# Two-layer diffusion backbone with expert retrieval: the opening and the last stage lead with token tile 0, context tile 0 moves into an earlier stage, and the modulation matmuls use four column tiles

## The chip, the cores and the metric

One core of a Trainium2 chip runs the whole forward pass as one program. The metric is the device time of that program in microseconds (us). The program is written out by hand: every engine (TensorE = PE, VectorE = DVE, ScalarE = ACT, GpSimd = POOL, SyncE = SP) has its own in-order list of instructions, and they meet at semaphores.

## The reference, cut to what matters

Batch 1, 256 latent tokens and 256 context tokens of width 1024, two layers, all in float32.

```python
for l in range(2):
    ada_x = (silu(c) @ w_ada[l] + b_ada[l])        # six vectors of 1024: modulation; ada_c the same from c_ctx
    hx = modulate(rms_norm(x, norm1_g[l]), ada_x[0], ada_x[1])
    hc = modulate(rms_norm(ctx, norm1_g[l]), ada_c[0], ada_c[1])
    # layer 0: short conv and gated chunk MLP on x and on ctx
    # layer 1: conformer conv, and differential attention of x over [ctx; x]; no new ctx
    yx, yc = mixer(hx, hc)
    x = x + ada_x[2] * yx
    x = x + ada_x[5] * peer(modulate(rms_norm(x, norm2_g[l]), ada_x[3], ada_x[4]))
    # layer 0: the same two lines for ctx

def peer(h):    # for each token: 8 heads x 16 experts out of 16384
    s = product_key_scores(h @ wq)                 # 2 x 128 scores per head
    idx, g = top16(s), softmax(...)
    act = gelu(sum(h * u_tab[idx])) * g
    return sum(act * v_tab[idx])                   # 128 gathered rows of u and v for each token
```

## The kernel before

**Tiles and stages.** Tokens lie on the 128 partitions, so each stream has two tiles (0 and 1). The three uses of `peer` are three stages: stage 0 is x in layer 0, stage 1 is ctx in layer 0, stage 2 is x in layer 1. A stage has 256 slots, 128 for tile 0 and then 128 for tile 1. In one slot POOL issues an indirect gather (L771) that brings one row of 2048 floats (u and v of one expert) to each of the 128 partitions, 1 MB in all, into one of eight ring rows `uv`. DVE multiplies the u half with the token and sums it (L1265), ACT makes the weight and a diagonal matrix of it (L902, L904, L906), and two slots later PE adds the v half to the accumulator with four matmul instructions (L716, `add_values`). POOL may refill a ring row once PE has used it (`uv_used`), and it needs `idx`, the chosen experts of the next head: head h feeds slots 16h to 16h+15 of each tile.

**What makes idx.** For a head: `query` (two groups of 8 matmuls, L548), `score` (L693), and `find`, a chain of small DVE instructions in six parts (L1207 to L1243). `find` runs for one tile or for both at once. `idx` is written at L1237.

**Order of the work.** `schedule()` writes one list that all engines walk. The list `before` (L148) has what runs ahead of a stage's first slot, with nothing gathered meanwhile: the *opening* ahead of stage 0 (modulation of layer 0 as ten `ada` pairs, mixer of x, out projection, first head), and ahead of stage 2 what I call the *last opening* (context norm, context keys and values, attention of 8 tile-heads, out projection, norm, first head). Everything else is `placed`: `spread` deals steps over slots by the costs in `SHARE`, and they run between the slots, while rows are gathered. Each engine takes its steps in list order, so a step that waits holds up the slots behind it on that engine.

**Weights.** SP loads the 118 weight blocks (1 MB each) in the order of first use. There are three slots in `wring`, and in the opening the eight rows of `uv` serve as well. A block's slot is free when its matmuls are done (`multiplied`, L739). POOL's first gather waits once for the last block that lies in `uv` (L777). Behind a query block SP also loads that head's keys, and waits for the `score` of two heads back (L745).

**Modulation.** `ada_pair` (L472) multiplies two blocks with `silu_c`, two columns wide (own and context vector): 16 matmuls of 128x256, which the compiler makes 32 instructions, the two blocks in two column positions (output partitions 0 and 32) at the same time. DVE copies two pieces of two partitions (L942, L943), `ada_turn` (L489) turns them with four matmuls (eight instructions).

**Attention** (L600 and L1138): for each of 8 tile-heads, PE makes scores (L615), DVE a maximum (L1143), ACT the exponentials (L842), DVE the difference of the two softmaxes (L1153), PE turns it (L623), ACT copies it, PE multiplies with the values (L629), and DVE scales the result into `orow` (`take_values`, L1134) before it mixes the next one.

## Time and profile before

| | |
|---|---|
| median of 3 runs | 2508.52 us (2507.24 to 2511.49) |
| the profiled execution, its own time | 2511.18 us |
| its span in the profile | 2509.4 us |
| first gather of stage 0 issued at | 220.08 us |
| last gathers of stage 1 landed, stage 2's first one issued | about 1689 us and 1842.68 us |
| HBM read | 935.88 MB |

How to read it: the span of the profile is what its stretches add up to; the time of an execution is 1.8 us longer, for what lies around the span. All times of rows are counted from the span's start. Busy times of engines overlap.

### The profile page before, as it was taken

Reading aid. Unit: us, or ns where it says so; the run is one execution under the profiler, and the core shown is the slowest. Engines: PE = TensorE matmul, PEld = TensorE weight load, DVE = VectorE, ACT = ScalarE, POOL = GpSimd, SP = SyncE. Lnnn points to the kernel's source line nnn. Section 1 sums busy time; section 2 is a strip of 40 time slices with the busy share of each in tenths; the row PEclk is TensorE's granted clock in tenths of the full one; section 3 lists DMA queues with packets and bytes.
Section 4 is the critical chain, followed back from the end, with each engine's and each line's share of the span. In section 5 each row is a group of like instructions: output and inputs, shape, how many; then the busy total and the mean of one; then the engine's idle time right before and its main releaser. Section 6 shows DMA issues by size and latency. Waiting matters only on the chain.

```text
span 2509.4 us, 23860 instructions
## 1 busy us (share of the span) xinstructions
PE 2162.3 (86%) x6888; PEld 1134.4 (45%) x6888; DVE 1557.4 (62%) x3791; ACT 907.8 (36%) x2688; POOL 1036.9 (41%) x868
## 2 busy tenths in 40 slices
PE   6997998889999978889799898897679987778777
PEld 4775544336655534444365443336455432222222
DVE  1326787775465568867847867454478887544444
ACT  1003343343233444433453334232234443333333
POOL 0002344344444444533434443420025445677774
PEclk9999999999999999999999999998789999999999
DMA  9516999999999999999999999982179999999997
GB/s 398 222 63 241 420 421 418 421 421 421 405 418 420 407 421 414 416 421 406 422 421 412 421 421 416 415 352 70 36 285 420 421 421 421 421 422 422 421 417 325
DMA packets 132304, 938.35 MB, mean 374 GB/s; under 512 B 14688, under 2 KB 17760, under 8 KB 18656
## 3 DMA queue, kind: packets, MB, share of 16 engines
q0 software_dynamic: 110592, 805.36, 77.7%
q1 hardware_dynamic: 21600, 131.63, 13.1%
q8 instruction: 55, 0.90, 0.1%
q14 instruction: 57, 0.47, 0.0%
HBM read 935.88 MB, written 1.05 MB: 373 GB/s over the span
## 4 chain that ended last, share of the span: by engine, by line
PE 41%; DMA 26%; DVE 13%; POOL 9%; issue 8%; ACT 3%; POOLq 0%; SPq 0%; DVEq 0%; ACTq 0%
DMA uv<-uv_dram,stage_idx 25%; PE psum L716 19%; PE psum L548 10%; POOL uv L771 8%; PE psum L535 6%; DVE uv L1265 5%; PE psum L482 2%; PE psum L665 1%; DMA uv<-ada_dram 1%; ACT diag L906 1%; DVE work L1231 1%; ACT wv L904 1%; DVE work L1233 0%; PE psum L496 0%; PE psum L629 0%
## 5 line engine op out<-in xcount | busy, mean ns | idle before, releaser
L716 PE MATMUL psum<-uv,diag 128*128 128x512 f32 x3072 | 1465.0, 617 | 258.2 <-ACT diag L906 251.0
L771 POOL DMA_INDIRECT uv<-uv_dram,stage_idx x768 | 1002.9, 1306 | 1069.1 <-PE psum L716 858.0
L1265 DVE CUSTOM_DVE_ANT_0 uv<-uv,h 128x1024 f32<-128x1024 f32 x768 | 931.7, 1224 | 543.8 <-DMA uv<-uv_dram,stage_idx 531.7
L716 PEld LDWEIGHTS psum<-uv,diag 128*128 128x128 f32 x3072 | 561.7, 193 | 1055.5 <-ACT diag L906 543.4
L902 ACT ACTIVATE gel<-dots 128x1 f32<-128x1 f32 x768 | 155.1, 202 | 1110.4 <-DVE dots L1265 1105.4
L906 ACT ACTIVATE diag<-const,wv 128x128 f32<-128x128 f32 x768 | 308.3, 401 | 25.0
L548 PE MATMUL psum<-hT,wring 128*128 128x256 f32 x1248 | 287.9, 386 | 3.7 <-ACT hT L811 3.7
L548 PEld LDWEIGHTS psum<-hT,wring 128*128 128x128 f32 x1248 | 241.6, 194 | 64.5 <-issue 29.5
L904 ACT ACTIVATE wv<-gel,gw 128x1 f32<-128x1 f32 x768 | 226.3, 295 | 24.9
L763 POOL COPY stage_idx<-idx 128x8 uint32 x96 | 33.9, 353 | 380.5 <-DVE idx L1237 379.8
L793 ACT ACTIVATE work<-psum 128x256 f32<-128x256 f32 (+1 forms) x110 | 47.0, 429 | 177.7 <-PE psum L548 138.1
L482 PE MATMUL psum<-wring,silu_c 128*2 128x256 f32 x544 | 69.6, 395 | 2.2 <-DMA wring<-ada_dram 2.2
L942 DVE COPY ada_rows<-psum 2x256 f32<-2x256 f32 x24 | 9.9, 411 | 96.6 <-PE psum L482 96.6
L1175 DVE TENSOR_TENSOR work<-psum,gate_mix 128x256 f32<-128x256 f32 (+1 forms) x24 | 12.3, 513 | 86.4 <-PE psum L535 57.1
L1265 DVE DVE_READ_ACCUMULATOR2_ANT dots<- 128x1 f32 x768 | 62.6, 82 | 0.0
L535 PE MATMUL psum<-wring,hT 128*128 128x256 f32 x256 | 57.9, 379 | 0.0
L535 PEld LDWEIGHTS psum<-wring,hT 128*128 128x128 f32 x256 | 48.6, 190 | 13.4 <-issue 7.4
L1068 DVE SCALAR_TENSOR_TENSOR work<-work,const 128x256 f32<-128x256 f32 x120 | 50.0, 477 | 0.0
L902 ACT ACT_TABLE_LOAD x38 | 48.8, 1283 | 0.7
L482 PE MATMUL psum<-uv,silu_c 128*2 128x256 f32 x224 | 33.3, 414 | 16.6 <-DMA wring<-ada_dram 10.9
L482 PEld LDWEIGHTS psum<-wring,silu_c 128*2 128x2 f32 x544 | 25.6, 87 | 44.7 <-issue 18.2
L1207 DVE MAX8 work<-work 128x8 f32<-128x128 f32 x96 | 21.2, 278 | 35.2 <-ACT work L793 35.1
(166 smaller groups left out, 1297.0 us busy)
## 6 DMA issues: line engine op xcount, KB each, us to landing
wring<-ada_dram SPq DMA_DIRECT2D x34, 1024.0 KB
wring<-in_dram SPq DMA_DIRECT2D x27, 1024.0 KB
wring<-wq_dram SPq DMA_DIRECT2D x24, 1024.0 KB
uv<-ada_dram SPq DMA_DIRECT2D x14, 1024.0 KB, 8.6
uv<-uv_dram,stage_idx POOLq DMA_INDIRECT x768
uv<-in_dram SPq DMA_DIRECT2D x7, 1024.0 KB, 22.0
uv<-out_w_dram SPq DMA_DIRECT2D x4, 1024.0 KB, 6.0
wring<-out_w_dram SPq DMA_DIRECT2D x4, 1024.0 KB
```

The source lines that it names most:

```text
L482: last = mm(bank[32 * i:32 * i + 2, 0:BLK], silu_c[:, k, :], kc(("ada", i))[:, k, :], start=(k == 0), stop=(k == KC - 1))
L535: last = mm(bank[:, 0:BLK], src[:, k, t * P:(t + 1) * P], w[:, k, :], start=(k == 0), stop=(k == KC - 1))
L548: last = mm(bank[:, 0:TOK], w[:, k, i * P:(i + 1) * P], hT[:, k, :], start=(k == 0), stop=(k == KC - 1))
L716: last = mm(acc[:, b, :], diag[:, s % RING, :], uv[:, s % RING, D + 512 * b:D + 512 * (b + 1)], start=(c == 0), stop=(c == NSEL - 1))
L763: nc.gpsimd.tensor_copy(stage_idx[:, half, :], idx[:, stage % 2, t, bass.ds(it * TOPK + half * RING, RING)]).then_inc(staged, 1)
L771: nc.gpsimd.indirect_dma_start(out=uv[:, s, :], out_offset=None, in_=tables[stage // 2], in_offset=bass.IndirectOffsetOnAxis(ap=stage_idx[ ...
L793: mine.emptied(f(dst, src, func, **kw))
L902: f(gel[:, r:r + 1], dots[:, r:r + 1], ACT.Gelu_apprx_tanh).then_inc(gelu_ready, 1)
L904: f(wv[:, r:r + 1], gel[:, r:r + 1], ACT.Copy, scale=gw[:, (T // TT) % 2, T % TT, c:c + 1]).then_inc(wv_ready, 1)
L906: f(diag[:, r, :], C("ident"), ACT.Copy, scale=wv[:, r:r + 1]).then_inc(diag_ready, 1)
L1068: ops = [v.scalar_tensor_tensor(out=ccT[:, j, :], in0=cpT[:, j, k:k + TOK], scalar=w[:, j, k:k + 1], in1=ccT[:, j, :], op0=ALU.mult, op1=A ...
L1265: v.tensor_tensor_reduce(out=uv[:, r, 0:D], in0=uv[:, r, 0:D], in1=h2[:, stage % 2, t, :], scale=1.0, scalar=0.0, op0=ALU.mult, op1=ALU.ad ...
```

## The change

1. **Opening, tile 0 first.** The out projection runs for tile 0 alone (`out_rows(0, 0)`), then come norm, turn back, query, score and find of head 0 for tile 0 (128 tokens), and then the out projection's remaining blocks, norm and turn back of tile 1. The query of head 1 (first half) is the last step ahead of slot 0.
2. **Last opening, tile 0 first.** Context tile 0 leaves it: its norm, key rows (`kc0`) and value rows (`vc0`) stand in stage 1's slots 131 to 246, beside `k_rows` and `x_rows`, and use the same weight blocks. Only context tile 1 stays. After attention step 5 come tile 0's out projection, norm and query, between the attention steps of tile 1; then score and find of tile 0; then the rest for tile 1.
3. **First heads by tile** (`heads_by_tile`): in stages 0 and 2, heads 0 to 2 of tile 1 are found apart from those of tile 0, within slots 6 to 30. `idx_ready` becomes one semaphore for each tile.
4. **Four column tiles for modulation.** `silu_c` is padded with zeros to 32 columns; `ada_pair` still has 16 matmuls, now in four column positions, each for half of the contraction of one block. One DVE copy of 128x256 takes the place of two small ones; `ada_turn` is two matmuls against a 0/1 matrix that also adds the halves.
5. **Attention:** ACT scales the values into `orow` in place of DVE, through its own ring of banks; from head 3 of tile 0 on the scores have one pair of banks, so that DVE's three banks are free for the out projection.
6. **Smaller ones:** the `spatial` steps are dealt among `ah_cols` and `ac_cols`; some scratch tiles move; `gate(2, 1)` goes from slots 20 to 40 to slots 40 to 60.

The core of the diff:

```diff
-        0: ada(0, 0, 2) + ... + gate(0, 0)
-        + project_out(0)[:4] + ada(0, 8, 9) + project_out(0)[4:] + rms(0) + ada(0, 9, 10) + [("mods", 0, 1)] + norm(0, 1)
-        + first_heads(0),
+        0: ada(0, 0, 2) + ... + gate(0, 0) + deal(out_rows(0, 0), ada(0, 8, 10)) + [("mods", 0, 1)]
+        + rms(0, (0,)) + out_rows(0, 1)[:1] + norm(0, 1)[:1] + [("turn_back", 0, 0)] + query(0, 0, (0,)) + score(0, 0, (0,))
+        + find(0, 0, (0,)) + out_rows(0, 1)[1:]
+        + rms(0, (1,)) + norm(0, 1)[1:] + [("turn_back", 0, 1)] + query(0, 1)[:1],
+        2: rms(1, (1,)) + [("norm_ctx", 2, 1)] + [("kc1", 2, b, 0) for b in range(2)] + [("kc_norm", 2, 1)]
+        + [("vc1", 2, b, 0) for b in range(2)] + [("kc_turn", 2, 1)]
+        + [("attend", 2, i) for i in range(HEADS + 2)] + [("o_norm", 2, 0), ("o_turn", 2, 0)]
+        + [("out_half", 2, 1, 0, 0), ("attend", 2, HEADS + 2), ("out_half", 2, 1, 1, 0)] + rms(2, (0,))
+        + [("attend", 2, HEADS + 3)] + norm(2, 1)[:1] + [("turn_back", 2, 0)] + query(2, 0, (0,))[:1]
+        + [("attend", 2, TT * HEADS), ("o_norm", 2, 1)] + query(2, 0, (0,))[1:] + [("o_turn", 2, 1)] + score(2, 0, (0,))
+        + find(2, 0, (0,)) + [("out_half", 2, 1, b, 1) for b in range(2)]
+        + rms(2, (1,)) + norm(2, 1)[1:] + [("turn_back", 2, 1)] + query(2, 1)[:1],
...
+def heads_by_tile(stage):
+    one, two = (0,), (1,)
+    return [(0, 6, query(stage, 1)[1:] + score(stage, 1, one) + find(stage, 1, one)),
+            (6, 12, query(stage, 0, two) + score(stage, 0, two) + find(stage, 0, two)),
+            (12, 18, query(stage, 2) + score(stage, 2, one) + find(stage, 2, one)),
+            (18, 24, score(stage, 1, two) + find(stage, 1, two) + query(stage, 3)),
+            (24, 30, score(stage, 2, two) + find(stage, 2, two) + query(stage, 4) + score(stage, 3)),
+            (30, 39, next_head(stage, 3))]
...
-                for k in range(KC):
-                    for i in range(2):
-                        last = mm(bank[32 * i:32 * i + 2, 0:BLK], silu_c[:, k, :], kc(("ada", i))[:, k, :],
-                                  start=(k == 0), stop=(k == KC - 1))
+                for k in range(KC // 2):
+                    for q in range(QUAD):
+                        i, kq = q // 2, q % 2 * (KC // 2) + k
+                        last = mm(bank[QW * q:QW * (q + 1), 0:BLK], silu_c[:, kq, :], kc(("ada", i))[:, kq, :],
+                                  start=(k == 0), stop=(k == KC // 2 - 1))
...
-                pool.wait_ge(idx_ready, it * TT + (stage * PH * TT + t + 1))
+                pool.wait_ge(idx_ready[t], it + (stage * PH + 1))
...
-                if i > 1:
-                    take_values(i - 2)
...
+                    empty(orow[:, t, h * P:(h + 1) * P], P, scale=prec[:, (i - 1) % 2, 0:1])
```

## Rows read from the trace of the kernel before

**Rows 1.** The page: busy shares and the span in 40 slices.
```profile
PE 2162.3 (86%) x6888; PEld 1134.4 (45%) x6888; DVE 1557.4 (62%) x3791; ACT 907.8 (36%) x2688; POOL 1036.9 (41%) x868
...
DMA  9516999999999999999999999982179999999997
```
**Rows 2.** Windows, core 0: start:end, length, busy of PE, PEld, DVE, ACT, POOL, PEclk, DMA share, GB/s.
```profile
0.00:220.00 220.00, 188.91 (x1040) 141.81 (x1040) 60.98 (x189) 26.30 (x52) 0.39 (x5) 0.96 0.53 207
220.00:1690.00 1470.00, 1320.78 (x4098) 686.12 (x4099) 1001.09 (x2435) 581.16 (x1732) 636.74 (x575) 0.97 1.01 415
1690.00:1842.00 152.00, 112.67 (x503) 85.30 (x501) 65.67 (x151) 41.93 (x93) 0.19 (x1) 0.85 0.17 59
1842.00:2485.00 643.00, 524.61 (x1218) 216.06 (x1219) 418.87 (x1004) 252.08 (x790) 397.89 (x287) 0.98 1.01 419
```
**Rows 3.** Waits by total, of the two gatherless stretches: POOL.
```profile
POOL stage_idx L763 <- DVE idx L1237: 218.4, 1, 218.4
POOL stage_idx L763 <- DVE idx L1237: 161.4, 1, 161.4
```
**Rows 4.** Timeline of PE in the opening: start, duration, instruction.
```profile
158.74 3.62 PE L482 MATMUL psum<-uv,silu_c 128*2 128x256 f32 x32
163.38 1.05 PE L496 MATMUL psum<-const,ada_rows 2*128 2x2 f32 x8 [1.01 <-DVE ada_rows L943]
144.83 13.98 PE L535 MATMUL psum<-uv,work 128*128 128x256 f32 x64
187.51 1.97 PE L519 MATMUL psum<-const,work 128*128 128x128 f32 x16
```
**Rows 5.** Timeline of PE: two column positions start side by side.
```profile
119.33 0.38 PE L482 MATMUL psum<-uv,silu_c 128*2 128x256 f32 x1
119.34 0.38 PE L482 MATMUL psum<-wring,silu_c 128*2 128x256 f32 x1
119.55 0.38 PE L482 MATMUL psum<-uv,silu_c 128*2 128x256 f32 x1
```
**Rows 6.** Timeline of DVE: find of one tile, from its first to its index instruction.
```profile
209.82 0.49 DVE L1207 MAX8 work<-work 128x8 f32<-128x128 f32 x2 [18.34 <-ACT work L793]
218.42 0.17 DVE L1237 SCALAR_TENSOR_TENSOR idx<-work 128x16 uint32<-128x16 f32 x1
```
**Rows 7.** Timeline of POOL: first gather, ninth and sixteenth.
```profile
220.08 1.09 POOL L771 DMA_INDIRECT uv<-uv_dram,stage_idx  x1 [1.04 <-issue]
234.20 0.96 POOL L771 DMA_INDIRECT uv<-uv_dram,stage_idx  x1 [3.53 <-PE psum L716]
261.60 0.94 POOL L771 DMA_INDIRECT uv<-uv_dram,stage_idx  x1 [5.42 <-PE psum L716]
```
**Rows 8.** Timeline of PE in the last opening, and of DVE at the first find.
```profile
1705.39 30.83 PE L535 MATMUL psum<-wring,uv 128*128 128x256 f32 x128 [1.57 <-ACT uv L811]
1737.84 0.71 PE L615 MATMUL psum<-h 64*128 64x256 f32 x4 [0.74 <-ACT uv L793]
1768.76 0.66 PE L623 MATMUL psum<-const,uv 128*128 128x128 f32 x4 [3.84 <-DVE uv L1153]
1789.20 16.03 PE L665 MATMUL psum<-wring,work 128*128 128x512 f32 x32 [0.69 <-ACT work L793]
1815.77 7.14 PE L548 MATMUL psum<-hT,wring 128*128 128x256 f32 x32 [1.58 <-ACT hT L811]
...
1832.39 0.68 DVE L1207 MAX8 work<-work 128x8 f32<-128x128 f32 x2 [16.72 <-ACT work L793]
```
**Rows 9.** The DMA view of 1690 to 1842 us.
```profile
DMA packets 1734, 9.00 MB, mean 59 GB/s; under 512 B 192, under 2 KB 704, under 8 KB 704
```
**Rows 10.** Windows, the first 100 us of gathers in stages 0 and 2, and stage 1's end.
```profile
220.00:320.00 100.00, 86.97 (x303) 47.16 (x304) 79.22 (x257) 37.35 (x108) 42.57 (x41) 0.95 1.01 416
1842.00:1942.00 100.00, 84.16 (x249) 46.73 (x250) 86.84 (x279) 40.16 (x118) 47.71 (x44) 0.93 0.99 407
1420.00:1690.00 270.00, 240.55 (x713) 112.02 (x712) 163.18 (x309) 102.11 (x308) 107.48 (x100) 0.96 1.00 408
```

More of the change, by code:

```diff
@@ L103, in project_even @@
     return (blocks_of(stage, "v_rows") + [("v_sum", stage)] + blocks_of(stage, "u_cols")[:2] + [("v_scale", stage)]
-            + blocks_of(stage, "u_cols")[2:] + blocks_of(stage, "ah_cols", "ac_cols")
-            + [("spatial", stage, t, j) for t in range(TT) for j in range(MC)] + blocks_of(stage, "ab_cols"))
-def project_out(stage):
-    return blocks_of(stage, "out_rows", n=D // BLK)
-def query(stage, h):
-    return [("query", stage, h, q) for q in range(2)]
-def find(stage, h, tiles):
+            + blocks_of(stage, "u_cols")[2:]
@@ L117, in find, with out_rows, query, score @@
+            + deal(blocks_of(stage, "ah_cols", "ac_cols"), [("spatial", stage, t, j) for t in range(TT) for j in range(MC)])
+            + blocks_of(stage, "ab_cols"))
+def out_rows(stage, t):
+    return [("out_rows", stage, b, t) for b in range(D // BLK)]
+def query(stage, h, tiles=(0, 1)):
+    return [("query", stage, h, q, tiles) for q in range(2)]
+def score(stage, h, tiles=(0, 1)):
+    return [("score", stage, h, tiles)]
+def find(stage, h, tiles=(0, 1)):
     return [("find", stage, h, tiles, part) for part in range(FIND_PARTS)]
@@ L526, in wait_hT, with token_major @@
                 pe.wait_ge(dve_took, n["hT"][1])
-            def token_major(banks, src, what, t):
-                if t == 0:
+            def token_major(banks, src, what, new, done):
+                if new:
                     weights(what)
@@ L534, in token_major, with tile, channel_major @@
                 for k in range(KC):
-                    last = mm(bank[:, 0:BLK], src[:, k, t * P:(t + 1) * P], w[:, k, :], start=(k == 0), stop=(k == KC - 1))
+                    last = mm(bank[:, 0:BLK], src[:, k, :], w[:, k, :], start=(k == 0), stop=(k == KC - 1))
                 banks.fill(last)
-                if t == TT - 1:
+                if done:
                     block_done(what, banks)
-            def channel_major(banks, what, i):
+            def tile(src, t):
+                return src[:, :, t * P:(t + 1) * P]
+            def channel_major(banks, what, i, tiles=(0, 1)):
+                tokens = slice(tiles[0] * P, (tiles[-1] + 1) * P)
                 if i == 0:
                     wait_hT()
-                    weights(what)
+                    if tiles[0] == 0:
+                        weights(what)
                 bank = banks.open(pe)
@@ L598, in qk_turn, with attention_scores @@
                 turn_heads(qk[:, t, :])
+            def attention_scores(i):
+                t, h = i // HEADS, i % HEADS
+                for m in range(2):
+                    half = slice(m * HD, (m + 1) * HD)
+                    for k, keys_of in enumerate((kxT, kcT)):
+                        last = mm(score_bank(i)[:, m, k * TOK:(k + 1) * TOK], qT[half, h, t * P:(t + 1) * P],
+                                  keys_of[half, h, :], start=True, stop=True)
+                last.then_inc(scores_full, 1)
             def attend(stage, i):
@@ L1188, in find @@
             def find(stage, h, tiles, part):
-                if part == 0 and tiles[0] == 0:
-                    n.up("scores")
-                k = n["scores"]
+                k = stage * PH + h + 1
                 a, b = tiles[0], tiles[-1] + 1
@@ L1329 @@
         "lam": rows_(f(d_lambda)),
+        "gather_sums": np.stack([[p // QW // 2 == i and p % QW == v for i in range(2) for v in range(2)] for p in range(P)])
+        .astype(np.float32),
         "b_spatial": np.repeat(f(b_spatial_b)[0].reshape(MC, 2, P).transpose(1, 0, 2), P // 2, axis=0).reshape(P, -1),
```

315 lines of the change are left out of this document (167 added, 148 removed).

## The prediction

> **What bounds the kernel now.** I read the page first: TensorE is busy 86% of the span, yet the line of DMA digits is at 9 everywhere except in slices 2 to 4 and around slice 29 [rows 1]. The windows say why. From 220 to 1690 us and from 1842 to 2485 us the DMA engines are full at 415 and 419 GB/s; in the opening they move 207 GB/s and between 1690 and 1842 us only 59 GB/s [rows 2]. In these two stretches nothing is gathered: the waits of POOL show that it stood 218.4 and 161.4 us for DVE's first index [rows 3]. So the time is (a) the two stretches ahead of a first index, set by a chain over PE, DVE and ACT, (b) bytes divided by some 417 GB/s, (c) a tail. A block or a gathered row of 1.049 MB costs 2.5 us at this rate. A change is worth what it takes off (a), less the blocks that were loaded in (a) and then have to be loaded in (b), plus what it makes (b) lose. The bytes themselves stay: 118 blocks and 768 gathers.
>
> **Opening, modulation.** One `ada` pair takes PE 3.62 us for 32 instructions, 113 ns each [rows 4]. The trace shows two column positions 10 ns apart and a new pair of instructions every 0.21 us [rows 5]; a lone stream of the same shape takes 13.98 / 64 = 218 ns for each [rows 4]. Going from one to two positions thus halved the time; no row shows four. Bounds: 1.8 us a pair (16 instructions' time halved again) to 3.62 us (no gain), or somewhat above. I take 1.8, since the nearest rows are themselves a doubling that worked. DMA sets pairs 0 to 3, of which only the last counts (1.8 plus its turns and copies, 3.0 together); pairs 4 to 7 give 4 x 1.8 = 7.3. `ada_turn` halves from 1.05 us [rows 4]: four of them, 2.0. Dealing out `spatial` saves a PE stall of 0.8. Up to the out projection: 13.1 us earlier.
>
> A rule speaks against this. The Trainium skill (TensorE: Matmul & The Clock Gate, Part 1) says that the sequencer may need about 62 ns for every matmul; counted for the weight loads too that would be 64 x 62 ns = 4.0 us a pair however many positions there are. By that sentence the pair would gain nothing and the opening would be some 12 us longer than I say.
>
> **Opening, tile 0 first.** From the start of the out projection (144.83) to the norm's transposes (187.51) the old path takes 42.7 us [rows 4]. The new one: four out steps and the first of tile 1, 5 x 3.5; two pairs, 3.6; two turns, 1.0; together 22, so 20.7 less. The norm statistics of tile 0 (about 3 us) lie beside tile 1's first step. From the transposes to the start of find (209.82) it was 22.3 us [rows 4, 6]. New: 8 transposes 1.0, their modulation 1.7, turning back 1.0, the query as 32 instructions of 128 columns at 1.97/16 = 0.123, 3.9, and copies and score 1.6: 9.2, so 13.1 less. Find itself stays at 8.6 us [rows 6]. Sum: 13.1 + 20.7 + 13.1 = 47, first gather near 173 instead of 220.
>
> The single wait of POOL for a block in `uv` moves to the third out block, which PE finishes for tile 1 near 169, while DVE still searches until 171.5. That cover is only 2 us. `idx_ready` split in two costs nothing: each tile's finds are in order on DVE.
>
> **Last opening.** Eight context steps take 30.83 us [rows 8]; four stay, near 3.85 each. With one tile less in the norm (2.7) attention begins 19 us earlier. From the first score (1737.84) to find (1832.39) the old path is 94.5 us [rows 8], of it 51.4 attention up to the out projection. Now attention of both tiles is still ahead of find, since tile 1's last steps stand before score; but tile 1's out projection, norm and query are not. Attention 51.4, less 1.6 as the scaling leaves DVE's serial chain; out projection of tile 0, 2 x 4.0; two adds 2.8; norm statistics 2.9; norm 2.7; turning back 1.0; query 3.9; score and copies 1.6: 72.7. DVE handles tile 1's softmax between these in program order and PE idles at every turn; the transposed probability of step 5 waited 3.84 us already [rows 8], and PEclk is 0.85 in this stretch [rows 2], that is, partly at the lower of its two levels. I allow 0 to 9 us for it and take 4, giving 77, so 17.5 less. Sum: 36, bounds 30 to 42. ACT's 0.35 us for each scaling lies beside DVE's maximum of the next step.
>
> **Blocks loaded later.** The old opening moves 207 GB/s x 220 us = 45.5 MB: constants, inputs and 40 blocks. At 173 us the new one has 36, because two query blocks stay held in the three slots: 4 x 2.5 = 10 us go back. Between 1690 and 1842 us 9.00 MB move [rows 9], 8 blocks; the new stretch loads 4, and 2 more beside find, when tile 1's out steps free their slots: 5 us go back (up to 10). Net so far: 47 + 36 - 15 = 68 us.
>
> **What the gather phase loses.** In the first 100 us of gathers DVE is busy 79.2 us in stage 0 and 86.8 in stage 2 [rows 10]. The change adds tile 1's adds, statistics and modulation, about 7 us, and finds by single tile where two were found at once, under one more find of 9.2 us; I take 6. DVE then stands at 92 and 100 of 100 us, with waits on top: find of head 1 can't begin before query 1 is done on PE, near 190 us, ten us behind its first dot. Against it stands the ring: eight rows are issued in 10 us and take 20 us to land, and in the old start DMA stayed full (416 GB/s) though rows 9 to 16 were issued only every 3.9 us [rows 7, 10]. I take 7 us lost in each of the two starts, bounds 0 and 18.
>
> The first query block of head 0 is held until slot 7, so the second block of `ada` pair 10 is issued only then, and SP's next query block and keys queue behind it; PE waits there about 5 us (1 MB at half the rate) with the values of slot 7 behind it. Eight rows in flight cover this: nothing, up to 5 if they have run out. In stage 2 query block 1 likewise waits for tile 1's out projection; its cover is the norm of tile 1.
>
> Stage 1 gets four more steps of 3.5 us on PE (14 us), and norm, transposes and copies of one context tile; the fourteen later pairs give back 1.8 us each. PE is at 240.6 of 270 us there [rows 10]; slack is 29 us, and DMA there runs at 408. I take 1 us, bounds -3 and 10. `gate(2, 1)`, the moved scratch tiles and the dealt `spatial` of stage 1 cost nothing: closing tile 0 needs the gate only at slot 128.
>
> **Sum.** 68 - 14 - 1 = 53 us off. The sum is against the profiled execution: 2511.2 - 53 = 2458. The median lies 2.7 us below that execution, which gives **2456 us**.
>
> **The rivals.**
> *A. Four positions gain nothing.* For it: no row shows an instruction faster than 113 ns, and eight tiny matmuls of two columns still take 1.05 us, 131 ns each [rows 4]. Against it: those load 128 columns each, and the pair's two streams start side by side. Eight places in the opening lose 1.8 us, less a little: 12 us, giving 2467 or 2468. The skill's sentence above is this case.
> *B. VectorE paces the starts.* For it: 100 of 100 us. Against it: the ring's 20 us. If rows come 25 us late in sum beyond my 14: 2481.
> *C. Slower than before.* The same mechanism at its extreme, in one place: the first 40 slots of stages 0 and 2, where finds by tile and dots alternate on DVE. If the old pace of rows 9 to 16, 3.9 us a row [rows 7], held for 40 rows in both stages with the ring empty, it would cost 2 x 40 x 1.4 = 112 us against 68: 2552. It decides the sign from 3.35 us a row on. Against it: DVE's work there is about 120 us for 40 rows, 3.0 a row, beside 48 transfers of 2.5 us that take just as long.
> *D. The change doesn't shorten the path.* The gather still waits, for the block in `uv` or for something of tile 1; then little but the modulation is left: within a few us of 2508. No such wait is in the code that I find.
>
> **How the numbers follow.** Chances: forecast 0.60 (own range 2440 to 2468), A 0.20, B 0.15, C 0.03, D 0.02. The low end takes 42 us for the last opening and hardly a loss at the starts, 53 + 6 + 12 = 71, so 2437; the high end takes in A and B: 2481. A measurement of this kernel can tell about 0.2%, 5 us, from no change. Faster by more: 0.95; within: 0.02; slower: 0.03.
>
> **What would show it.** First gather near 173 us and the last stage's near 1806 counted on the old clock, that is some 115 us after the last value of stage 1 instead of 149. L482: 1.8 us a pair and a new wave of four every 0.21 us (A: 3.6). The windows of the first 100 us of gathers: DMA above 390 GB/s (B: below 370, with DVE at 95 or more and POOL waiting for `idx`). Stage 1's last 270 us: PE busier, DMA still at about 408. I am wrong if a first gather comes more than 10 us later than said, or if gathers in the middle run below 410 GB/s.

## The result, and the profile after

The changed kernel takes 2474.23 us in the median of 4 runs (2471.97 to 2484.66), beside 2507.88 for the kernel before in the same session: ratio 0.9873, 95% interval 0.9842 to 0.9903. That is 33.6 us off; forecast were 53, down to 2456. The profiled execution was the fastest of its four, 2471.97 us with a span of 2470.2, so span against span the change gives 39.2 us. The other 5.6 us between the two differences are which execution happened to be profiled: the one before lay 3.3 us above the median of 2507.88, the one after 2.3 below its own.

The page shows the shorter opening and the shorter hole in the DMA digits; the 8 ahead of the hole (slice 27) was there before too. Compare [rows 1].

```profile
PE 2116.3 (86%) x6856; PEld 1125.4 (46%) x6856; DVE 1559.2 (63%) x3849; ACT 937.2 (38%) x2734; POOL 1027.7 (42%) x868
...
DMA  9629999999999999999999999982199999999997
```

The windows of the same four stretches (columns as in [rows 2]):

```profile
0.00:170.60 170.60, 142.56 (x908) 114.63 (x908) 51.49 (x164) 23.63 (x44) 0.39 (x5) 0.97 0.61 245
170.60:1664.00 1493.40, 1330.85 (x4248) 712.07 (x4248) 1015.64 (x2498) 603.96 (x1774) 630.38 (x575) 0.97 1.00 411
1664.00:1782.00 118.00, 82.00 (x328) 57.63 (x328) 51.19 (x124) 38.55 (x82) 0.19 (x1) 0.74 0.13 44
1782.00:2445.00 663.00, 545.04 (x1340) 235.64 (x1340) 429.74 (x1050) 264.60 (x813) 394.79 (x286) 0.98 1.00 411
```

Two things are new: the second stretch is 23 us longer and the fourth 20 us longer than before, at 411 GB/s instead of 415 and 419; and the granted clock of the last opening is 0.74, not 0.85. POOL's waits for a first index, against the 218.4 and 161.4 us of [rows 3]:

```profile
POOL stage_idx L826 <- DVE idx L1305: 168.9, 1, 168.9
...
POOL stage_idx L826 <- DVE idx L1305: 128.8, 1, 128.8
```

For every kernel below the span is cut at the same four points of POOL's timeline: first gather; last gather of stage 1 issued (the start of the second wait); first index copy of stage 2; last gather issued.

| us | to first gather | stages 0 and 1 | second wait | PEclk in it | stage 2 | median |
|---|---|---|---|---|---|---|
| before | 220.1 | 1460.1 | 161.4 | 0.85 | 643.2 | 2507.88 |
| after | 170.6 | 1481.6 | 128.8 | 0.74 | 664.5 | 2474.23 |
| difference | -49.5 | +21.5 | -32.6 | | +21.3 | -33.6 |

So the two openings gave 82 us and the two gather phases took 43 back. Each row is one profiled execution. How far one can be trusted is seen where the same code recurs: the ten kernels below that share the changed kernel's path up to the first gather have it at 170.9 to 173.7 us. Stages 0 and 1 with the same steps give 1481.6 and 1481.4, but 1485.0 with some of them left out. Stage 2 with the new order gives 664.5, 665.4 and 665.6, with the old one 643.2, 643.2 and 643.8. Stage 2 can be read to 1 us, stages 0 and 1 only to about 4. A kernel's executions as a whole differ by more, 12.7 us for the changed one, and only one of each is in this table.

The opening in PE's timeline of the changed kernel (compare [rows 4]):

```profile
85.17 1.93 PE L524 MATMUL psum<-uv,silu_c 128*32 128x256 f32 x32
...
128.75 1.46 PE L575 MATMUL psum<-uv,work 128*128 128x256 f32 x6
...
151.44 1.09 PE L559 MATMUL psum<-const,work 128*128 128x128 f32 x8 [0.23 <-DVE work L1065]
...
159.11 0.71 PE L753 MATMUL psum<-keys,work 128*128 128x128 f32 x4 [0.37 <-ACT work L856]
```

A modulation pair takes 1.93 us instead of 3.62; the out projection begins 16.1 us earlier, the norm's transposes 36.1, the scores that start find some 49.

And the first gathers, first, ninth and sixteenth (compare [rows 7]):

```profile
170.63 1.09 POOL L834 DMA_INDIRECT uv<-uv_dram,stage_idx  x1 [1.04 <-issue]
...
192.84 1.15 POOL L834 DMA_INDIRECT uv<-uv_dram,stage_idx  x1 [10.35 <-PE psum L779]
...
219.72 0.94 POOL L834 DMA_INDIRECT uv<-uv_dram,stage_idx  x1 [6.83 <-PE psum L779]
```

The ninth comes 22.2 us after the first, where it took 14.1 before: the ring is full and waits for the first value step. Why is seen in three timelines of the same 20 us. DVE, whose first dot (L1333) stands behind tile 1's statistics and modulation, and which then stands still for 9.28 us until ACT has copied head 1's scores (L856), though rows lie ready:

```profile
177.12 1.36 DVE L1071 TENSOR_SCALAR hT<-psum,modg,ada_c 128x128 f32<-128x128 f32 x4 [2.06 <-PE psum L559]
178.52 1.23 DVE L1333 CUSTOM_DVE_ANT_0 uv<-uv,h 128x1024 f32<-128x1024 f32 x1
...
190.76 0.49 DVE L1274 MAX8 work<-work 128x8 f32<-128x128 f32 x2 [9.28 <-ACT work L856]
```

ACT, whose gelu of that dot (L979) stands behind the copy of query 1 (L856), for which it waits:

```profile
185.71 0.38 ACT L856 ACTIVATE work<-psum 128x256 f32<-128x256 f32 x1 [4.55 <-PE psum L593]
...
187.41 0.20 ACT L979 ACTIVATE gel<-dots 128x1 f32<-128x1 f32 x1
```

And PE, whose first value (L779) stands behind all of query 1 (L593) and its scores (L753):

```profile
180.32 8.81 PE L593 MATMUL psum<-hT,wring 128*128 128x256 f32 x32
189.60 0.71 PE L753 MATMUL psum<-keys,work 128*128 128x128 f32 x4 [0.47 <-ACT work L856]
190.15 3.60 PE L779 MATMUL psum<-uv,diag 128*128 128x512 f32 x8
```

A row thus passes three in-order engines, and a query or a find on one of them holds it up on all. This reading was put to the test below, and it is only part of the price.

### The profile page after: what moved, and what is told of

It is laid out like the page before. It is cut to its first block, busy times and chain, and to the rows that moved or that the text cites. A ratio compares the mean times of both kernels' runs of the same rounds, so it can differ in the third digit from the quotient of the medians.

```text
span 2470.2 us, 23913 instructions
## 1 busy us (share of the span) xinstructions
PE 2116.3 (86%) x6856; PEld 1125.4 (46%) x6856; DVE 1559.2 (63%) x3849; ACT 937.2 (38%) x2734; POOL 1027.7 (42%) x868
## 4 chain that ended last, share of the span: by engine, by line
PE 44%; DMA 22%; DVE 13%; POOL 8%; issue 8%; ACT 4%; POOLq 0%; SPq 0%; DVEq 0%; ACTq 0%
PE psum L779 22%; DMA uv<-uv_dram,stage_idx 20%; PE psum L593 11%; POOL uv L834 8%; PE psum L575 6%; DVE uv L1333 5%; PE psum L524 1%; PE psum L725 1%; DMA wring<-ada_dram 1%; ACT diag L983 1%; DMA uv<-ada_dram 1%; ACT wv L981 1%; PE psum L685 1%; PE psum L753 1%; ACT gel L979 0%
## 5 line engine op out<-in xcount | busy, mean ns | idle before, releaser
L779 PE MATMUL psum<-uv,diag 128*128 128x512 f32 x3072 | 1470.5, 619 | 255.7 <-ACT diag L983 250.6
L834 POOL DMA_INDIRECT uv<-uv_dram,stage_idx x768 | 992.4, 1292 | 1121.2 <-PE psum L779 906.5
L1333 DVE CUSTOM_DVE_ANT_0 uv<-uv,h 128x1024 f32<-128x1024 f32 x768 | 933.1, 1226 | 530.2 <-DMA uv<-uv_dram,stage_idx 521.5
L779 PEld LDWEIGHTS psum<-uv,diag 128*128 128x128 f32 x3072 | 566.1, 194 | 1047.5 <-ACT diag L983 525.2
L979 ACT ACTIVATE gel<-dots 128x1 f32<-128x1 f32 x768 | 154.8, 202 | 1053.6 <-DVE dots L1333 1052.6
L593 PE MATMUL psum<-hT,wring 128*128 128x256 f32 (+1 forms) x1280 | 280.8, 374 | 0.0
L593 PEld LDWEIGHTS psum<-hT,wring 128*128 128x128 f32 x1280 | 238.7, 195 | 61.2 <-issue 34.1
L856 ACT ACTIVATE work<-psum 128x256 f32<-128x256 f32 (+2 forms) x126 | 51.6, 410 | 201.8 <-PE psum L593 134.1
L1333 DVE DVE_READ_ACCUMULATOR2_ANT dots<- 128x1 f32 x768 | 63.4, 83 | 0.0
L1020 DVE COPY ada_rows<-psum 128x256 f32<-128x256 f32 x24 | 10.2, 424 | 82.3 <-PE psum L524 82.2
L524 PE MATMUL psum<-wring,silu_c 128*32 128x256 f32 x560 | 41.5, 414 | 19.9 <-DMA wring<-ada_dram 18.5
L575 PEld LDWEIGHTS psum<-wring,hT 128*128 128x128 f32 x256 | 48.7, 190 | 13.4 <-issue 7.4
L1274 DVE MAX8 work<-work 128x8 f32<-128x128 f32 x96 | 21.6, 281 | 52.6 <-ACT work L856 52.6
L593 PE MATMUL psum<-hT,uv 128*128 128x256 f32 x192 | 43.1, 380 | 0.0
L954 ACT ACT_TABLE_LOAD x31 | 39.8, 1283 | 0.5
## 6 DMA issues: line engine op xcount, KB each, us to landing
uv<-uv_dram,stage_idx POOLq DMA_INDIRECT x768, 14.1
```

Of the source, the lines that this page charges most:

```text
L524: last = mm(bank[QW * q:QW * (q + 1), 0:BLK], silu_c[:, kq, :], kc(("ada", i))[:, kq, :], start=(k == 0), stop=(k == KC // 2 - 1))
L575: last = mm(bank[:, 0:BLK], src[:, k, :], w[:, k, :], start=(k == 0), stop=(k == KC - 1))
L593: last = mm(bank[:, 0:len(tiles) * P], w[:, k, i * P:(i + 1) * P], hT[:, k, tokens], start=(k == 0), stop=(k == KC - 1))
L779: last = mm(acc[:, b, :], diag[:, s % RING, :], uv[:, s % RING, D + 512 * b:D + 512 * (b + 1)], start=(c == 0), stop=(c == NSEL - 1))
L834: nc.gpsimd.indirect_dma_start(out=uv[:, s, :], out_offset=None, in_=tables[stage // 2], in_offset=bass.IndirectOffsetOnAxis(ap=stage_idx[ ...
L856: mine.emptied(f(dst, src, func, **kw))
```

## The experiments

First the parts of the change, one by one. Ratios are to the kernel before in the same session, with the 95% interval.

### e1: two column positions again

```diff
-                for k in range(KC // 2):
-                    for q in range(QUAD):
+                for k in range(KC):
+                    for i in range(2):
...
-                mine.emptied(v.tensor_copy(ada_rows[:, pair % 2, :], bank[:, 0:BLK]))
+                v.tensor_copy(ada_rows[:, pair % 2, 0, :], bank[0:2, 0:BLK])
+                mine.emptied(v.tensor_copy(ada_rows[:, pair % 2, 1, :], bank[32:34, 0:BLK]))
```

> The changed kernel with the old modulation: two column positions, two small copies, four turns a pair. Theory (the opening is a chain on TensorE, and each microsecond of it counts in full): a pair takes 3.6 us again in place of 1.9, a turn 1.05 in place of 0.5, so the first gather comes 12 to 14 us later (183 to 185 us) and the total rises by 11 to 14 us over the changed kernel. Rival (what the columns give in the opening is mostly hidden behind transfers or given back in stage 0): the first gather moves, the total rises by under 5 us.

Measured: 2498.76 us, ratio 0.9955 (0.994 to 0.997), so the columns are worth 24.5 us between the medians and 21 between the ratios, nearly twice what rival A gave them, and more than the 11 to 14 that were expected here. First gather 190.4 (19.8 later, 12 to 14 were expected), stages 0 and 1 1487.2 (5.6 longer, near the scatter), second wait and stage 2 as in the changed kernel (129.1 and 665.6). Its pair:

```profile
114.30 3.62 PE L523 MATMUL psum<-wring,silu_c 128*2 128x256 f32 x32
```

Four positions nearly halve 3.62 to 1.93: 64 instructions, loads included, in 1.93 us, 30 ns each. In the pair that the changed kernel runs from 64.54 us on, a wave of four matmuls starts every 0.22 us, 55 ns a matmul.

The Trainium skill (TensorE: Matmul & The Clock Gate, Part 1) puts about 62 ns of sequencer time on a matmul where hardware decode is off. This trace has less than that by either count, 30 ns with the loads, as the prediction counted them for its rival, and 55 ns for the matmuls alone; no run shows how decode was set.

### e2: the old order of the opening

The opening's list, and the heads of stage 0, as before; columns and last opening stay.

```diff
-        0: ... + gate(0, 0) + deal(out_rows(0, 0), ada(0, 8, 10)) + [("mods", 0, 1)]
-        + rms(0, (0,)) + out_rows(0, 1)[:1] + norm(0, 1)[:1] + ...
+        0: ... + gate(0, 0)
+        + blocks_of(0, "out_rows", n=4)[:4] + ada(0, 8, 9) + blocks_of(0, "out_rows", n=4)[4:] + rms(0) + ada(0, 9, 10)
+        + [("mods", 0, 1)] + norm(0, 1) + first_heads(0),
```

> The changed kernel, but its opening in the old order with both tiles ahead, and stage 0's heads placed as before; last stage and columns as changed. Theory (the early start pays, less the blocks handed on and less an underfed start): first gather near 206 us, 35 later; DMA back above 412 GB/s in the first 150 us of gathers in place of 381; the total rises by only 12 to 20 us. Rival (the underfed start has nothing to do with the order of tiles, the find work as such is too much for VectorE): DMA stays near 380 and the total rises by 30 us or more.

Measured: 2478.49 us, 0.9879 (0.9862 to 0.9895). First gather 203.4, 32.8 later; but stages 0 and 1 take 1460.0, as before (1460.1), and DMA moves 418 GB/s in the first 150 us of gathers, where the changed kernel has 382. Tile 0 first in the opening wins 33 us and loses 21.6: the whole loss of stages 0 and 1 hangs on it, and stage 1's extra context steps cost nothing that can be seen. Net 4 us in the median, not the 12 to 20 that were expected, and the two intervals overlap. Part of the missing difference has nothing to do with the opening: the second wait of e2 is 4.6 us shorter than that of the changed kernel (124.2 against 128.8), with the same steps in it.

### e3: the old order of the last opening

Context tile 0 stays in stage 1, and the new attention too.

```diff
-        + [("attend", 2, i) for i in range(HEADS + 2)] + [("o_norm", 2, 0), ("o_turn", 2, 0)]
-        + [("out_half", 2, 1, 0, 0), ("attend", 2, HEADS + 2), ...
+        + [("attend", 2, i) for i in range(HEADS + 2)] + [("o_norm", 2, 0)]
+        + [("attend", 2, i) for i in range(HEADS + 2, TT * HEADS + 1)] + ... + rms(2) + norm(2, 1) + first_heads(2),
```

> The changed kernel, but the last stage's opening in the old order (attention of both tiles, then projection, norm and first heads of both tiles) and its heads placed as before; context tile 0 stays in stage 1, and the attention's new banks stay. Theory: from the last value of stage 1 to the first gather of stage 2 it takes 128 to 132 us in place of 118, but 8 blocks are loaded in it in place of 4 and the start is fed in full, so that the total is 3 to 10 us lower than the changed kernel's: the last stage's tile order costs what it gives. Rival (the earlier gather pays in full): the total rises by 10 to 14 us.

Measured: 2472.89 us, 0.9859 (0.9843 to 0.9876), no slower than the whole change; the 3 to 10 us less that were expected are not there either (1.3, and the intervals overlap). The wait is 146.9 us, 18.1 longer than in the changed kernel, and 136.0 us from last value to first gather instead of the expected 128 to 132, but stage 2 is back at 643.2, 21.3 shorter. Tile 0 first in the last stage gains nothing on the whole.

### e8: context tile 0 back in the last opening

e3 with this in addition:

```diff
-        2: rms(1, (1,)) + [("norm_ctx", 2, 1)] + [("kc1", 2, b, 0) for b in range(2)] + [("kc_norm", 2, 1)]
+        2: rms(1) + [("norm_ctx", 2, t) for t in range(TT)] + [("kc%d" % t, 2, b, 0) for b in range(2) for t in (1, 0)]
+        + [("kc_norm", 2, 0), ("kc_norm", 2, 1)] + ...
```

> The kernel of e3_old_last (new opening, new attention, old order of the last opening), with context tile 0's norm, keys, values and key norm taken out of stage 1 and put back ahead of the attention of the last opening; both tiles share the four blocks. If moving context tile 0 is what shortened the wait from 161.4 to 146.9 us in e3, the wait goes back to 160 to 163 and stages 0 and 1 get 2 to 4 us shorter (1481.4 in e3): 2482 to 2486 in all. If the new attention order did it (fewer turns to and fro between the engines), the wait stays at 146 to 150 and the whole within 2470 to 2475.

Measured: 2489.58 us, 0.992 (0.9904 to 0.9937). The wait is 162.8 us, the 161.4 of before; stage 2 643.8. The move of context tile 0 is worth 16 us of wait and 16.7 of the median; the new attention alone shortens nothing. Stages 0 and 1 did not get shorter without its steps (1485.0), though 2 to 4 us were expected, so that the time lies 4 us above the expected 2482 to 2486.

### e4: tile 1's preparation behind the gathers

The first test of the reading above: norm and turn of tile 1 and query 1 leave the opening. Beside the lines shown, head 2 and the modulation of slots 3 to 100 start some slots later, and POOL's first gather waits for the last out projection block in `uv` alone.

```diff
-        + find(0, 0, (0,)) + out_rows(0, 1)[1:]
-        + rms(0, (1,)) + norm(0, 1)[1:] + [("turn_back", 0, 1)] + query(0, 1)[:1],
+        + find(0, 0, (0,)) + out_rows(0, 1)[1:],
...
-    return [(0, 6, query(stage, 1)[1:] + score(stage, 1, one) + find(stage, 1, one)),
+    return [(0, 3, rms(stage, two) + norm(stage, 1)[1:] + [("turn_back", stage, 1)] + query(stage, 1)[:1]),
+            (3, 8, query(stage, 1)[1:] + score(stage, 1, one) + find(stage, 1, one)),
```

> The changed kernel, but norm statistics, norm, turning back of tile 1 and the query of head 1 go from ahead of slot 0 to slots 0 to 3 in stages 0 and 2, head 1 of tile 0 to slots 3 to 8, and what follows is shifted by two slots. Theory (the starts are underfed because the first values stand behind tile 1's norm and both query halves on TensorE, and VectorE waits 9 us for head 1's scores): the ninth gather comes within 14 us of the first in place of 22, DMA in the first 150 us rises from 381 to above 395 GB/s, and the total falls by 8 to 16 us. Rival (VectorE has too much to do in the first 40 slots): the same work is done later, DMA stays at 375 to 385, the total moves by under 3 us.

Measured: 2485.68 us, 0.99 (0.9884 to 0.9917), 11 us slower than the changed kernel, where 8 to 16 less were expected; stages 0 and 1 1497.7, stage 2 672.7, the ninth gather 23.2 us after the first. The stages are read from an execution of 2495.58 us, 10 above the median, so that about half of their excess is that execution's. Slots 0 to 3 are still ahead of or among the first values, so this tested the order badly, and it pushed head 1's index later. e9 does it properly.

### e9: head 1 of tile 0 scored in the opening, tile 1's norm behind the first values

```diff
-        + rms(0, (1,)) + norm(0, 1)[1:] + [("turn_back", 0, 1)] + query(0, 1)[:1],
+        + query(0, 1, (0,)) + score(0, 1, (0,)),
...
+    return [(1, 7, find(stage, 1, one)),
+            (3, 12, rms(stage, two) + norm(stage, 1)[1:] + [("turn_back", stage, 1)] + query(stage, 0, two)
+             + score(stage, 0, two) + query(stage, 1, two) + find(stage, 0, two)),
```

The last opening and stage 2 get the same, and the modulation of slots 3 to 100 starts at slot 12.

> The changed kernel, but tile 0's query and scores of head 1 (3.6 + 0.6 us of TensorE) stand in the opening and in the last opening, where TensorE waits for VectorE, and tile 1's norm, turn and queries stand in slots 3 to 12, behind the first values (before: ahead of them). The first dot of the changed kernel ran at 178.5 though its row had landed by 173, and its value at 190.2. If the order at the start is what costs, the ninth gather comes 14 us after the first instead of 22 and each start gets back 4 to 8 us: 2462 in all. If it is the amount of work in the first 40 slots, the total stays: the first values come sooner, but the rows of slots 10 to 40 come as late as now, 2470 to 2476.

Measured: 2467.31 us, 0.9826 (0.9809 to 0.9842). The ninth gather now comes 14.9 us after the first, as expected, but the twelfth 30.2 (after: 29.0); stages 0 and 1 take 1483.9 and stage 2 666.8, no shorter. The order theory fell as far as it was about the first values: what was saved ahead of them was lost a few slots on. DVE stands as long for scores as before, 21.0 and 21.4 us in the first 150 us of the two starts (after: 21.2 and 23.3); the table below shows what that is worth. What e9 gained is in the second wait, 120.1 us instead of 128.8, and that goes with the clock (below).

### e5, e6, e7, e11: less work in the starts

e5 takes one pair of query blocks out of the first 40 slots, with nothing left out. e6 and e7 leave work out to weigh one engine each: e6 copies tile 0's lists for tile 1, e7 runs two of eight products. e11 has both.

```diff
 e5
-    q = query(stage, h + 2) if h + 2 < PH else [None, None]
+    q = query(stage, h + 1)
+    return [f[0], q[0], f[1], f[2], q[1], f[3], f[4]] + score(stage, h + 1) + [f[5]]
 e6
+                if stage != 1 and tiles == (1,):
...
+                        v.tensor_copy(idx[:, stage % 2, 1, h * TOPK:(h + 1) * TOPK],
+                                      idx[:, stage % 2, 0, h * TOPK:(h + 1) * TOPK]).then_inc(idx_ready[1], 1)
 e7
+                n_k = 2 if short else KC
```

> The changed kernel, but in stages 0 and 2 the queries run one head ahead instead of two: the first 40 slots of each hold one pair of query blocks (7.2 us of TensorE) less. Rows leave the ring only through TensorE, so if the starts are short because TensorE has more work there than the transfers last (127 us busy of the first 150), each start gets back 5 to 7 us: first gather where it was (170 and 1781), stages 0 and 1 1475 us instead of 1481.6, stage 2 658 instead of 664.5, 2462 in all. If VectorE's finds are what holds the starts (115 to 120 us busy of the first 150), the time stays within 2471 to 2477.

> The changed kernel, but tile 1's lists of heads 0, 1 and 2 in stages 0 and 2 are not searched: tile 0's indices and weights are copied in their place, so tile 1's experts of these heads are the wrong ones and VectorE has some 30 us less to do in the first 30 slots of each stage. TensorE's work and all transfers are unchanged. If VectorE's finds hold the starts, each gets back 10 us or more: 2450 to 2455. If TensorE's work does, under 3 us each: 2469 to 2475.

> The changed kernel, but in stages 0 and 2 the queries of heads 1 to 5, and of tile 1 of head 0, run two of their eight products (so the wrong experts are chosen): TensorE has some 30 us less in the first 40 slots of each (5 x 7.2 and 3.6 us, three quarters), nothing else is changed. If TensorE's work holds the starts, nearly their whole price goes: stages 0 and 1 1468 to 1471 us instead of 1481.6, stage 2 650 instead of 664.5, 2448 in all; the opening and last opening are 2 us shorter too (query(1) of tile 1). If VectorE's finds do, under 3 us each: 2469 to 2475.

> e6_copied_finds and e7_short_queries at once (wrong experts, for both reasons). Alone, 30 us less of VectorE in each start gave back 8.6 and 7.8 us (stages 0 and 1; stage 2), 30 us less of TensorE 5.7 and 9.1. If the two engines' work stands in turn, row by row, the gains add: stages 0 and 1 1467 to 1469 us instead of 1481.6, stage 2 647 to 649 instead of 664.5, 2436 in all. If each alone already reaches what the transfers allow, they don't: 1472 and 655, 2452.

| us | stages 0 and 1 | second wait, PEclk | stage 2 | median | ratio |
|---|---|---|---|---|---|
| after | 1481.6 | 128.8, 0.74 | 664.5 | 2474.23 | 0.9873 (0.9842 to 0.9903) |
| e5 (PE -7 us a start) | 1483.9 | 124.4, 0.81 | 661.4 | 2468.84 | 0.9832 (0.9812 to 0.9852) |
| e6 (DVE -30) | 1473.0 | 124.3, 0.78 | 656.7 | 2454.51 | 0.9786 (0.9766 to 0.9806) |
| e7 (PE -30) | 1475.9 | 126.8, 0.76 | 655.4 | 2454.09 | 0.9769 (0.9753 to 0.9785) |
| e11 (both) | 1475.2 | 119.4, 0.85 | 650.1 | 2443.72 | 0.9749 (0.9728 to 0.9769) |

None came out as expected for one engine alone: e5 fell between its two cases, e6 gave back 8 or 9 us a start where 10 or more or under 3 were expected, e7 6 and 9 where 11 to 15 or under 3 were, and e11 lies midway between its 2436 and 2452. So neither engine's work alone is the bound: 30 us less of either gives stage 2 back 8 or 9 us, both together 14.4, nearly the sum. In stages 0 and 1 they don't add (8.6, 5.7 and 6.4, in a figure good to 4 us).

Are the starts short because PE and DVE are both nearly full? The first 150 us of stage 2, each from its first gather on, in the kernel before, the changed one, e6, e7 and e11 (columns as above):

```profile
1842.00:1992.00 150.00, 130.00 (x384) 70.95 (x385) 128.90 (x406) 65.89 (x189) 72.43 (x66) 0.95 1.00 412
```
```profile
1782.00:1932.00 150.00, 127.23 (x432) 76.60 (x433) 119.96 (x384) 66.64 (x178) 62.21 (x56) 0.97 0.95 374
```
```profile
1772.00:1922.00 150.00, 134.62 (x461) 81.48 (x462) 102.70 (x300) 70.83 (x192) 65.10 (x59) 0.97 0.99 398
```
```profile
1776.00:1926.00 150.00, 115.35 (x324) 58.34 (x325) 129.03 (x413) 70.36 (x192) 63.31 (x61) 0.94 1.00 404
```
```profile
1768.00:1918.00 150.00, 117.33 (x337) 60.76 (x338) 107.94 (x310) 72.56 (x198) 66.65 (x63) 0.94 1.01 417
```

They are not: before, both engines did more in these 150 us (130 and 129 us, against 127 and 120), and DMA still moved 412 GB/s. What differs is what DVE waits for. Before and after, in the same two windows:

```profile
DVE uv L1265 <- DMA uv<-uv_dram,stage_idx: 16.8, 15, 3.5
...
DVE work L1274 <- ACT work L856: 23.3, 6, 8.9
...
DVE uv L1333 <- DMA uv<-uv_dram,stage_idx: 0.7, 1, 0.7
```

Before, DVE had time left and waited for rows, 16.8 us in sum, and never for scores. After, it waits 23.3 us for scores that ACT copies out of PE's bank, and hardly ever for a row (0.7 us): rows lie ready while it stands. `heads_by_tile` puts each of the first finds right behind its own score, and most of them right behind their query too, so in-order DVE waits at find while PE still multiplies, and the dots behind it wait as well. The old order has a head's query two heads ahead of its find and its score one (`next_head`). In eleven kernels, for the first 150 us of stage 2 (e1, e2 and e8 are as after, after and e3 there):

| | PE busy | DVE busy | DVE waits for scores | DVE waits for rows | GB/s | stage 2 |
|---|---|---|---|---|---|---|
| before | 130.0 | 128.9 | 0 | 16.8 | 412 | 643.2 |
| e3 (old order there) | 132.2 | 128.4 | 0 | 18.8 | 414 | 643.2 |
| e4 | 120.8 | 111.1 | 28.0 | 5.2 | 348 | 672.7 |
| after | 127.2 | 120.0 | 23.3 | 0.7 | 374 | 664.5 |
| e9 | 127.3 | 117.5 | 21.4 | 7.5 | 367 | 666.8 |
| e5 | 123.6 | 124.3 | 19.2 | 0.5 | 385 | 661.4 |
| e13 | 126.5 | 117.0 | 14.2 | 13.3 | 392 | 659.6 |
| e12 | 127.0 | 118.0 | 12.4 | 13.9 | 395 | 658.7 |
| e7 (PE -30) | 115.4 | 129.0 | 11.8 | 3.1 | 404 | 655.4 |
| e6 (DVE -30) | 134.6 | 102.7 | 33.2 | 5.9 | 398 | 656.7 |
| e11 (both) | 117.3 | 107.9 | 10.6 | 24.4 | 417 | 650.1 |

So DVE paces these starts, with its standing still counted: 120 us busy and 26 waiting for other engines. e7 shortens the waits, e6 the work beside them, and so the two nearly add. In stage 0 it is the same: 21.2 us of waiting for scores after, none before and in e2. No run took away this wait alone, so how much of the 12 us it is worth is not shown; by and large stage 2 gets shorter as it shrinks (e6 apart, which leaves searches out, and has 11.4 of its 33.2 us at the dots behind them).

### e12 and e13: the same work, later

In e12 nothing is left out. Tile 1 stays one head behind tile 0 through all eight heads, so that by slot 40 five half heads are found instead of eight, and each query stands just ahead of its scores; on top of e9.

```diff
+def heads_one_behind(stage):
...
+    for h in range(2, PH):
+        at = TOPK * h - 18
+        out += [(at - 6, at - 1, query(stage, h)), (at - 0.5, at + 8, score(stage, h) + find(stage, h, one)),
+                (at + 8, at + 15.5, find(stage, h - 1, two))]
+    return out + [(110, 118, find(stage, PH - 1, two))]
```

> The changed kernel, with the same work in stages 0 and 2 put later: head 1 of tile 0 scored in the openings as in e9, tile 1 one head behind tile 0 through all eight heads, each query just ahead of its scores. By slot 40 the finds run are 5 half heads instead of 8 (some 27 us of VectorE less) and the queries 2 fewer (14.5 us of TensorE less), with nothing left out. If the starts are short because this work stands ahead of the rows, row for row, it gives back 6 to 10 us in each of stages 0 to 1 (1472 to 1476) and 2 (655 to 659), and the last opening keeps e9's 120 to 124 us: 2448 to 2455 in all, the fastest of these kernels. If the work only moves the same loss to later slots, it stays at e9's 2467.

Measured: 2469.45 us, 0.9828 (0.9805 to 0.9852), not the expected 2448 to 2455 but what was said of a loss that only moves. Stage 2 is 658.7, 5.8 us shorter and within what was expected. Stages 0 and 1 are 1485.5, no gain where 6 to 10 us were expected. Its windows, over the start of stage 0 and the 300 us behind it (171 to 321 and 321 to 621), and then the same two of the changed kernel:

```profile
171.00:321.00 150.00, 123.58 (x480) 69.70 (x479) 110.30 (x347) 65.81 (x174) 56.95 (x55) 0.93 0.97 395
321.00:621.00 300.00, 264.51 (x886) 140.87 (x886) 215.83 (x620) 129.74 (x367) 124.09 (x113) 0.97 1.00 410
```
```profile
171.00:321.00 150.00, 127.38 (x495) 77.59 (x496) 114.72 (x376) 63.52 (x167) 52.94 (x51) 0.95 0.96 382
321.00:621.00 300.00, 265.98 (x857) 137.55 (x857) 203.99 (x522) 121.10 (x363) 132.43 (x120) 0.96 1.01 421
```

13 GB/s more for 150 us and 11 less for 300: in the second window DVE waits for rows only 38.7 us instead of 86.1, and the rest went to waits for PE and ACT. My reading is that in stage 0, where the gate and the next layer's modulation follow, the finds carried the loss with them, and that in stage 2 little else follows and there is room; no run separates the two. The modulation of slots 3 to 100 starts at slot 12 here too. So e13 takes stage 0 from e9 and e5, and stage 2 from e12:

```diff
-            for first, last, steps in heads_by_tile(stage):
+            for first, last, steps in (heads_by_tile if stage == 0 else heads_one_behind)(stage):
```

> Stage 0 as in e9_head1_in_opening with the queries one head ahead (e5_one_ahead), stage 2 as in e12_one_behind; all work is there. If the parts keep what they gave alone: first gather 171.9, stages 0 and 1 1481 to 1484 us, last opening 120 to 128, stage 2 659, so 2458 to 2465 in the median. If the gains of e9 and e5 in stage 0 were only the scatter of the runs, 2466 to 2470.

Measured: 2458.19 us (2457.63 to 2460.81, 5 runs), ratio 0.9797 (0.9783 to 0.981): the fastest kernel with all the work in it, 16 us under the changed one. First gather 170.9, stages 0 and 1 1480.4, second wait 120.6 at clock 0.84, stage 2 659.6. That is within the expected 2458 to 2465, and the interval lies below that of the changed kernel altogether. Of the 14 us by which its span is shorter, stage 2's 4.9 are the schedule's, 8.2 are the second wait, with its clock, and stages 0 and 1 are within their scatter.

### The clock of the last opening

The second wait of the eleven kernels with tile 0 first there runs from 119 to 129 us though their path is the same. Ordered by the granted clock of that stretch: 0.74 gives 128.8 and 129.1 (after, e1), 0.75 128.2 (e12), 0.76 126.8 (e7), 0.78 124.3 and 124.2 (e6, e2), 0.81 124.4 (e5), 0.82 124.1 (e4), 0.84 120.6 (e13), 0.85 120.1 and 119.4 (e9, e11). The mean mixes two levels, 1.2 and 2.4 GHz. The same two query groups of tile 0 in the changed kernel and in e9:

```profile
1759.84 3.62 PE L593 MATMUL psum<-hT,wring 128*128 128x128 f32 x16
...
1766.00 1.95 PE L593 MATMUL psum<-hT,wring 128*128 128x128 f32 x16
```
```profile
1756.39 1.95 PE L594 MATMUL psum<-hT,wring 128*128 128x128 f32 x16
...
1760.46 1.95 PE L594 MATMUL psum<-hT,wring 128*128 128x128 f32 x16
```

3.62 and 1.95 us for the same 16 instructions are the lower and the upper level. In both kernels PE had waited 6.69 us for DVE's softmax of tile 1 a few us earlier; when the clock rises again behind such waits differs from kernel to kernel by some us. Over the whole second wait PE is busy 92.2 us in the changed kernel and 83.9 in e9, for the same steps: 8.3 us of the 8.7 by which the waits differ. What is left, PE's idle time, is 36.0 to 36.6 us in all eleven kernels. So the 9 us are matmuls that took longer at the lower level, and hardly anything of them is schedule. What makes the clock differ stays open: no run set it on purpose, and it isn't shown whether it belongs to a kernel or to an execution.

## Why the prediction was right or wrong

Faster, and within the range of 2437 to 2481, but not by the forecast's size: the gains were right in sum (82 us against 83), the price was too low (43 against 30), and most of that in one term, the starts.

- **Modulation columns.** Forecast 1.8 us a pair and 13.1 us up to the out projection; measured 1.93 and 16.1. Taking the doubling on from [rows 5] was right, and the count of the Trainium skill's 62 ns for loads too did not hold here; [rows 4] already spoke against it, with 64 instructions in 3.62 us where it asks for 4.0. Rival A's size was too low as well: without the columns not 12 but 21 to 25 us are gone (e1), 19.8 of them ahead of the first gather. Six pairs at 1.69 and six turns at 0.55 make 13.4 of these; 3.8 more stand between the two kernels already at the first norm's transposes (36.66 and 40.45 us), where the prediction had 3.0 for the first four pairs; the rest I haven't traced.
- **Tile 0 first in the opening.** Forecast 33.8 more, first gather near 173; measured 33.4 more and 170.6. Right to 2.5 us in sum. The wait for the block in `uv` did not show.
- **Last opening.** Forecast 36 (30 to 42) from last value to first gather; measured 149.0 to 118.1, 30.9. Context tile 0 counts 16 of the forecast 19 (e8 against e3, at 0.87 and 0.80 of the clock), tile 0 first 18 of 17.5 (e3 against after). The 19 was an overcount: half of 30.83 and the 2.7 beside it make 18. The clock took more than the 5 us that are missing: I allowed 4 us for idle PE at 0.85, but after has 0.74. Where the clock stayed at 0.85, in e9, it was 109.2 us, 39.8 less than before.
- **Blocks loaded later.** Forecast 10 and 5 us. The opening moves 245 x 170.6 = 41.8 MB where it moved 45.5; the last opening 5.16 MB where it moved 9.00 [rows 9]. That is 3.5 and 3.7 blocks, 9 us each: nearly right for the first, too little for the second, where the upper bound of 10 was the one to take.
- **The starts: the step that failed.** Forecast 7 us in each of stages 0 and 2 (bounds 0 and 18), and 1 for stage 1. Of the 21.5 and 21.3 us, less 9 for blocks, 12 are left in each: 25 instead of 15. I argued that 120 us of DVE beside 48 transfers that last as long would do no harm, with eight rows of ring to cover the order. I set DVE's work against the transfers and left out its standing still. The one such wait that I named, for query 1 near 190 us, came as said (190.76), and the ring did not cover it; and such waits come back at six finds, 23.3 us in sum, in the first 150 us of stage 2, where the old order has none. DVE's 120 us of work were right, but with the waits it had no time left, and the rows waited for DVE. Rival B thus had the right place and the right engine, but not the cause: its test "DMA below 370, DVE at 95 or more of 100" was met only in half, and only in stage 2 (383 and 365 GB/s in the first 100 us, DVE busy 70.5 and 74.6), because DVE was not busy but stuck. My own sign, DMA above 390, failed in both starts.
- **Stage 1.** 14 us more of PE beside the gathers cost nothing seen: e2 has stages 0 and 1 at 1460.0, and the last 269 us of stage 1 move 400 GB/s, against 402 in the same stretch before. PE is not busier there (237 and 239 us).
- **Sum.** In the span: -49.5 - 32.6 + 18 + 25 = -39 against -53; and 5.6 us less gain in the median by the choice of the profiled execution.

What stays open: in stages 0 and 1 the 12 us are tied to the opening's order by e2 and eased by e6 and e7, but neither e9, e5 nor e12 got them back, though e12 had only 11.4 us of waiting for scores left in the start of stage 0, and the 6 to 9 us of e6 and e7 are near the scatter of that stretch.

## What to carry to other kernels

When a start-up is cut by doing half the work first, the other half lands at the start of the next phase: here 33 and 18 us won at the head came back as 21.6 and 21.3, blocks included. Price that start not by how full the engines are, but by how far each step stands behind what it waits for: the old order had PE and DVE busier and the transfers full, because its queries were done long before their finds; the new one put find right behind its query, and an in-order engine that stands at a find holds up every row behind it. And look at whether the moved work can go where little follows: in stage 2 later finds gave 5 us, in stage 0 none.

## What the runs showed of the hardware

- Four column positions run 64 PE instructions (32 matmuls of 128x256, 32 loads of 128x32) in 1.93 us, a wave of four every 0.22 us; two positions took 3.62 us for as many matmuls.
- The granted clock of the last opening, where PE waits up to 6.7 us at a time for DVE, was 0.74 to 0.85 for the same steps in eleven kernels, and moved its length by 9 us, more than most of the schedules that were tried; PE's idle time in it was 36.0 to 36.6 us in all of them. A difference of a few us between two such kernels is not to be put down to their schedule before that column is read.
